# RWKV units of a two-block forward pass: each engine's order laid out over two head pairs, with half-swapped operands

## Chip, cores and metric

One core of one Trainium2 chip. The metric is the device time of one launch in microseconds (us); lower is better. Engines are named as in the profile: PE is TensorE (PEld its weight loads), DVE VectorE, ACT ScalarE, POOL GpSimd, SP SyncE.

## What is computed

The launch runs two transformer-like blocks of two layers each on 512 positions of width 1024, in float32: attention layers first, then a block with an HGRN mixer, an RWKV-7 mixer, a Fourier mixer, a convolution and feed-forward layers. The change touches the RWKV-7 recurrence alone, 8 heads of width 64, run forward and backward in time:

```python
def step(state, inp):
    r_t, w_t, k_t, v_t, a_t, b_t = inp
    sa = jnp.einsum('bhvk,bhk->bhv', state, a_t)
    state = (state * w_t[:, :, None, :] + sa[..., None] * b_t[:, :, None, :]
             + v_t[..., None] * k_t[:, :, None, :])
    return state, jnp.einsum('bhvk,bhk->bhv', state, r_t)
...
for d, (wd, ad, reverse) in enumerate(((wd_f, ad_f, False), (wd_b, ad_b, True))):
    w = -jax.nn.softplus(-(w0[d] + jnp.tanh(wd) @ w2[d])) - 0.5
    decay = jnp.exp(-jnp.exp(heads(w)))
    a = jax.nn.sigmoid(heads(a0[d] + ad @ a2[d]))
    k_d = k_h * (1.0 + (a - 1.0) * k_a_h)
    args = (r_h, decay, k_d, v_h, -kk, kk * a)
    ...
    bonus = bonus + jnp.sum(r_h * k_d * r_k32, axis=-1, keepdims=True) * v_h
```

## The kernel before

The recurrence is cut into chunks of 64 positions. Inside a chunk it becomes a triangular system, which is solved with an inverse that is built by doubling; between chunks it becomes a chain of 8 small state steps. `rwkv_units` does the part inside the chunks, once for each direction d (tiles named ru0 for d = 0, ru1 for d = 1; the profile leaves the numbers out), and `rwkv_states` runs the chain after it. Each call of `rwkv_units` is a stage of its own, with a barrier before and after, and loops over four head pairs (PAIRS = 4). A tile holds one pair: 128 partitions are two halves of 64, and what stands in a half changes with the step: the two heads (index e), or the even and odd chunk of four chunk pairs (index j for the half, t for the chunk pair). Almost every matmul has 64x64 weights, so it uses one quarter of the array: input half times output half. Each float32 matmul leaves two records in the trace.

The steps for one pair, with the function that issues them and its line:

- **turn** (L2555, PE): transposes of the three operands ar, b and kd into banks 0, 1 and 2; **naturals** (L2722, L2726, L2728, ACT) copies them out.
- **scores** (L2568, PE): products of keys and receptances; **masks** (L2785, DVE) multiplies them with the causal masks into `sc`, in two parts k = 0 and k = 1; after part 0 comes the seed of the inverse, a predicated copy (L2792) and a 32x32-block transpose (L2796). `inv` holds the inverse twice: `inv[:, slot, 0]` transposed, `inv[:, slot, 1]` plain.
- **keyed_values** (L2580, PE), copied out by ACT at L2762.
- **level** 1 to 5 (LEVELS = 6): for both heads e, the factors (L2596, PE) are copied out by **taking** (L2717, ACT); the blocks (L2611, PE) multiply that copy with the inverse, in two products k = 0 and k = 1 (level 5 has only one); **adding** (L2805, DVE) puts them into `inv` where the level's mask allows it. The next level's factors need it. This ring PE, ACT, PE, DVE is the heart of a pair.
- **solve** (L2625, PE), copied by **results** (L2733, ACT); **reads** (L2643, PE) with **reading** (L2816, DVE) and **values** (L2737, ACT); **maps** (L2661, PE) with **offsets** (L2744, ACT) and **stepping** (L2822, DVE).
- The class `Decays` prepares the operands of the next pair meanwhile: **lows** (L2348, PE, four records), **tanhs** (L2357, ACT), **sums** (L2384 and the scan L2386, DVE), **difference** (L2393, DVE), **powers** (L2366, L2367, L2371, ACT), **keys** (L2409, L2410, L2412, DVE), **operands** (L2418, L2419, L2421, DVE), and **others** (L2401, L2430 or L2432, L2435, L2436, L2440, L2441, POOL).

Every engine's queue runs in the order in which the block functions write it; a wait holds back all that is behind it. Before the change, PE's order for pair i is turn(i), scores(i), solve(i-1), lows(next), keyed_values(i), level 1, reads(i-1), level 2, maps(i-1), levels 3 to 5. Thus only solve, reads and maps of the pair before stand inside a pair; turn, scores, masks and seed come at its front, with no level in flight. The last pair's solve, reads and maps follow after the loop.

## Time and profile before

| | us |
|---|---|
| median of 3 runs | 2653.24 (2646.54 to 2654.29) |
| profiled execution, its own time | 2654.18 |
| its span | 2652.3 |
| PE busy in the span | 2507.2 (95%) |
| DVE busy | 1564.7 (59%) |
| ACT busy | 958.9 (36%) |
| POOL busy | 326.6 (12%) |

How to read it: the span runs from the first to the last instruction, and the time of the run lies 1.9 us above it. The busy shares are means over all stages of the launch; the RWKV units are two stretches of about 120 us each, from 1356 to 1490 us and from 1503 to 1622 us of the span. A matmul's end in the trace is modelled, so PE's pace is read from the distance between starts.

### The profile page before, as it was taken

How to read it: one execution, taken by the hardware profiler on the slowest of the kernel's cores; microseconds unless marked ns; L12 is line 12 of the kernel's file. 1: busy time of each engine (PE TensorE's matmuls, PEld its weight loads, DVE VectorE, ACT ScalarE, POOL GpSimd, SP SyncE). 2: the span in 40 equal slices, each digit the busy share in tenths (PEclk: the TensorE clock that was granted, in tenths of full speed). 3: DMA queues.
4: the chain of work that ended last, by engine and by line, in shares of the span. 5: the costliest groups of instructions: out<-in, count | busy, mean ns of one | idle time of the engine just before them, and what ended most of it. 6: DMA issues, size and time to landing. Idle time of an engine off the chain costs nothing. (4 is left out here: it accounts for less than half of the span.)

```text
span 2652.3 us, 43599 instructions
## 1 busy us (share of the span) xinstructions
PE 2507.2 (95%) x18620; PEld 1987.2 (75%) x18620; DVE 1564.7 (59%) x2236; ACT 958.9 (36%) x1435; POOL 326.6 (12%) x255
## 2 busy tenths in 40 slices
PE   6999999999999999999889797999999998999998
PEld 5888766678887666788668785788878766788786
DVE  5375378753753787656456565955556696655532
ACT  5223224542232245543444243433322423433321
POOL 1000030030000300300242220300003101100011
PEclk9999999999999999999889998999999998999999
DMA  4333223133332231222100001432334212222231
GB/s 152 96 95 96 97 96 133 56 116 98 100 95 97 96 120 68 102 95 96 62 5 4 3 4 61 179 99 99 118 153 183 64 58 72 88 96 96 84 127 51
DMA packets 56992, 239.38 MB, mean 90 GB/s; under 512 B 6560, under 2 KB 7328, under 8 KB 48224
## 3 DMA queue, kind: packets, MB, share of 16 engines
q1 hardware_dynamic: 56800, 236.61, 25.6%
q8 instruction: 147, 2.41, 0.4%
q14 instruction: 45, 0.37, 0.0%
HBM read 232.39 MB, written 4.19 MB: 89 GB/s over the span
## 5 line engine op out<-in xcount | busy, mean ns | idle before, releaser
L471 PE MATMUL banks<-h,head 128*128 128x512 f32 x1776 | 415.5, 390 | 0.0
L471 PEld LDWEIGHTS banks<-h,head 128*128 128x128 f32 x1776 | 333.1, 188 | 68.8
L471 PE MATMUL banks<-h,pin_pair 128*128 128x512 f32 x1488 | 345.2, 391 | 0.0
L471 PEld LDWEIGHTS banks<-h,pin_pair 128*128 128x128 f32 x1488 | 278.5, 188 | 57.2
L471 PE MATMUL banks<-h,ff_pair 128*128 128x512 f32 x1296 | 298.3, 390 | 0.0
L471 PEld LDWEIGHTS banks<-h,ff_pair 128*128 128x128 f32 x1296 | 243.4, 188 | 50.3
L458 DVE TENSOR_TENSOR head<-first,head 128x1024 fp32r<-128x1024 f32 x74 | 90.5, 1223 | 106.6 <-ACT head L450 106.6
L3163 DVE TENSOR_TENSOR ff<-ff_c,ff 128x512 fp32r<-128x512 f32 x42 | 29.1, 692 | 203.3 <-ACT ff L3151 203.3
L471 PE MATMUL banks<-h,pab_pair 128*128 128x512 f32 x504 | 116.2, 390 | 0.0
L450 ACT ACTIVATE head<-first 128x1024 fp32r<-128x1024 f32 x74 | 78.3, 1058 | 91.9 <-PE banks L471 91.9
L471 PEld LDWEIGHTS banks<-h,pab_pair 128*128 128x128 f32 x504 | 94.6, 188 | 19.6
L458 DVE TENSOR_TENSOR pin_pair<-first,pin_pair 128x1024 fp32r<-128x1024 f32 x34 | 41.7, 1226 | 90.7 <-ACT pin_pair L450 90.7
L1444 DVE SCALAR_TENSOR_TENSOR x<-banks,modf,x 128x512 f32<-128x512 f32 x28 | 21.0, 749 | 114.5 <-PE banks L490 114.5
L458 DVE TENSOR_TENSOR pin_pair<-pin_raw,pin_pair 128x1024 fp32r<-128x1024 f32 x32 | 39.2, 1226 | 79.5 <-ACT pin_pair L450 79.5
L2805 DVE COPY_PREDICATED ru_inv<-b_rp,banks 128x512 f32<-128x512 uint32 (+1 forms) x80 | 53.4, 674 | 51.9 <-PE banks L2611 51.7
L3391 DVE SCALAR_TENSOR_TENSOR cd_acc<-b_hb,params,cd_acc 128x512 f32<-128x512 f32 x108 | 81.2, 752 | 3.6
L990 ACT ACTIVATE dil_pt<-banks 128x1024 f32<-128x1024 f32 x32 | 32.3, 1023 | 140.2 <-PE banks L861 109.4
L490 PE MATMUL banks<-ff,dn_low 128*128 128x512 f32 x352 | 82.4, 389 | 0.0
L207 POOL TENSOR_TENSOR acc<-dn_sq 128x512 f32<-128x512 f32 x2 | 9.3, 4672 | 564.8 <-ACT dn_sq L195 564.8
L490 PEld LDWEIGHTS banks<-ff,dn_low 128*128 128x128 f32 x352 | 66.1, 188 | 13.7
L406 PE MATMUL banks<-h,head 128*128 128x512 f32 x144 | 44.8, 454 | 28.4 <-PEq L70 28.4
L792 POOL MEMSET dil_negmax<- 96x512 bf16 x2 | 1.0, 521 | 569.0 <-POOLq L70 569.0
(590 smaller groups left out, 4910.2 us busy)
## 6 DMA issues: line engine op xcount, KB each, us to landing
first<-in_w_in SPq DMA_DIRECT2D x64, 512.0 KB, 3.5
first<-in_ffn_up SPq DMA_DIRECT2D x56, 512.0 KB, 3.7
dn_raw<-in_ffn_down SPq DMA_DIRECT2D x16, 1408.0 KB, 7.2
dil_ring<-in_ada_w SPq DMA_DIRECT2D x20, 1024.0 KB, 6.9
pin_raw<-in_w_in SPq DMA_DIRECT2D x32, 512.0 KB, 3.5
ff_raw<-in_ffn_up SPq DMA_DIRECT2D x28, 512.0 KB, 3.7
mla_ada_ring<-in_ada_w SPq DMA_DIRECT2D x12, 1024.0 KB, 9.2
first<-in_ab_in SPq DMA_DIRECT2D x22, 512.0 KB, 3.3
```

Source lines behind the costliest of these rows:

```text
L207: self.nc.gpsimd.tensor_tensor(self.m.acc[:, n], self.sq[:, 0, n] if k == 1 else self.m.acc[:, n], self.sq[:, k % 2, n], ALU.add).then_inc ...
L406: mm = nc.tensor.matmul(m.ps[:, 0], pair[0][a][:, k], self.to[:, b, k], start=k == 0 and i == 0, stop=k == KD - 1 and i == 2, skip_group_c ...
L450: nc.scalar.activation(pair[t % slots][0], ring.at(t), ACT.Copy).then_inc(rounded, 1)
L458: nc.vector.tensor_tensor(pair[t % slots][1], ring.at(t), pair[t % slots][0].bitcast(F32), ALU.subtract).then_inc(split, 1)
L471: mm = nc.tensor.matmul(bank, w(a, k), x(b, k), start=k == 0 and i == 0, stop=k == kt - 1 and i == 2)
L490: mm = nc.tensor.matmul(bank, w(1, k), x(0, k), start=False, stop=k == kt - 1)
L792: nc.gpsimd.memset(m.negmax[:], 0.0).then_inc(zeroed, 1)
L990: nc.scalar.activation(pt[:, s:s + 2], m.ps[:, s:s + 2], ACT.Exp, scale=scale)\
L1444: ins = nc.vector.scalar_tensor_tensor(m.x[:, j], m.ps[:, j % 4], gate[:, j:j + 1], m.x[:, j], ALU.mult, ALU.add)
L2805: nc.vector.copy_predicated(inv[:, i % 2, f:2, e], over(m.levels[:, d, l, f:2]), m.ps[:, 4 + e, 2 * f * P:].rearrange("p (k t n) -> p k t ...
L3163: chain.step(nc.vector.tensor_tensor(ff[:, 1, j], cv[:, j % 2], ff[:, 0, j].bitcast(F32), ALU.subtract))
L3391: ins = nc.vector.scalar_tensor_tensor(acc[:, k], hb[:, k, tap:tap + T], w[:, 4 * tap + k:4 * tap + k + 1], acc[:, k], ALU.mult, ALU.add)
```

## The change

It leaves the numbers of instructions of most steps as they are and does five things.

1. It splits `level` into `factors` and `blocks`, `turn` into two calls, and `masks` into its two parts, and writes every engine's order anew. PE's order for pair i is now lows(next), factors 1, solve(i-1), blocks 1, turn of ar and b, factors 2, turn of kd, keyed_values, blocks 2, factors 3, reads(i-1), blocks 3, maps(i-1), factors 4, blocks 4, factors 5, scores(i+1), blocks 5. scores(0) stands ahead of the loop.
2. Factors, keyed_values and solve read one half and write the other (`halves(1 - j)`). Blocks take product 0 from half s to half s and product 1 from half s to the other half r, in turn, where before both went from a half to the same half.
3. For that, ACT copies the seed into the swapped half (`cross`, two instructions of 64 partitions) and `naturals` copies ar in two instructions of 64 partitions instead of one of 128. The seed is made in `m.acc`; POOL's fill is half as large.
4. The banks of PSUM are given out anew: scores in 0 to 3, turn in 0 to 2, reads in 0 and 1, maps in 2 and 3, the levels in 4 to 7.
5. POOL's `others` waits for the tiles' release (turn, reading, diagonal) only behind its first two instructions; scores waits for the first two of POOL's five counts, turn for all five.

The core of the diff:

```diff
             nc.gpsimd.tensor_tensor(self.kds[:, i], self.kds[:, i], self.kd[:], ALU.add).then_inc(self.pooled, 1)
         pool.wait_ge(self.powered, 4 * n + 1)
+        if freed is not None:
+            freed()
...
+                        def freed():
+                            pool.wait_ge(turned, 3 * i + 3)
+                            if i >= 1:
+                                pool.wait_ge(readx, 2 * i - 1)
+                                pool.wait_ge(diag, i)
+
+                        dc.others(pool, i + first, *following(i), (i + 1) % 2, freed)
...
+                def turn(i, some):
                     if i + first:
                         pe.wait_ge(dc.ready, 3 * (i + first))
                         pe.wait_ge(dc.pooled, 5 * (i + first))
-                    if i == 0 and first:
...
                 def scores(i):
+                    if i + first:
+                        pe.wait_ge(dc.ready, 3 * (i + first))
+                    if i + first:
+                        pe.wait_ge(dc.pooled, 5 * (i + first - 1) + 2)
+                    if i == 0 and first:
+                        pe.wait_ge(dc.opened, 2)
                     if i >= 1:
-                        pe.wait_ge(added, 2 * (LEVELS - 1) * i)
+                        pe.wait_ge(natural, 4 * i)
+                        pe.wait_ge(akvx, i)
+                    if i >= 2:
+                        pe.wait_ge(readx, 2 * (i - 1))
+                        pe.wait_ge(qsx, i - 1)
+                        pe.wait_ge(ptx, i - 1)
...
+                def blocks(i, l):
+                    done = 2 * (LEVELS - 1) * i + 2 * (l - 1)
                     if l == 1:
-                        pe.wait_ge(akvx, i + 1)
+                        pe.wait_ge(crossed, 2 * i + 2)
                     for e in range(2):
                         pe.wait_ge(taken, done + e + 1)
-                        for k in range(2 if l < LEVELS - 1 else 1):
-                            for t in range(TT):
+                        for t in range(TT):
+                            at = 2 * P + t * RC
+                            for k in range(2 if l < LEVELS - 1 else 1):
                                 for j in range(2):
-                                    r = halves(j)
-                                    b, back = a1[r, e, t], inv[r, i % 2, 1, e, t]
-                                    lhs, rhs = ((b, back), (back, b))[k]
-                                    at = (1 - k) * 2 * P + t * RC
-                                    mm = nc.tensor.matmul(m.ps[r, 4 + e, at:at + RC], lhs, rhs,
-                                                          start=k == 0 and t == 0, stop=t == TT - 1,
-                                                          skip_group_check=True)
+                                    r, s = halves(j), halves(1 - j)
+                                    b, back = a1[s, e, t], inv[s, i % 2, 1, e, t]
+                                    if k == 0:
+                                        mm = nc.tensor.matmul(m.ps[s, 5 + 2 * e, at:at + RC], b, back, start=False,
+                                                              stop=t == TT - 1, skip_group_check=True)
+                                    else:
+                                        mm = nc.tensor.matmul(m.ps[r, 4 + 2 * e, at:at + RC], back, b, start=t == 0,
+                                                              stop=t == TT - 1, skip_group_check=True)
                         mm.then_inc(paired, 1)
 
                 def solve(i):
                     pe.wait_ge(added, 2 * (LEVELS - 1) * (i + 1))
                     pe.wait_ge(akvx, i + 1)
...
-                                r = halves(j)
-                                mm = nc.tensor.matmul(m.ps[r, 3 - e, t * P:t * P + P], inv[r, i % 2, 1, e, t],
-                                                      x[r, i % 2, e, t], start=t == 0, stop=t == TT - 1,
+                                s = halves(1 - j)
+                                mm = nc.tensor.matmul(m.ps[halves(j), 3 - e, t * P:t * P + P], inv[s, i % 2, 1, e, t],
+                                                      x[s, i % 2, e, t], start=t == 0, stop=t == TT - 1,
                                                       skip_group_check=True)
                         mm.then_inc(solved, 1)
...
                             .then_inc(gated, 1)
+                scores(0)
                 for i in range(PAIRS):
-                    turn(i)
+                    if following(i):
+                        pe.wait_ge(masked, 4 * i + 2)
+                        dc.lows(pe, *following(i), low_banks)
                     if d == 0 and i == 0:
                         pe.wait_ge(placed, PAIRS)
-                    scores(i)
+                    factors(i, 1)
+                    pe.wait_ge(masked, 4 * i + 4)
                     if i >= 1:
                         solve(i - 1)
+                    blocks(i, 1)
                     if following(i):
-                        pe.wait_ge(natural, 3 * i + 2)
-                        dc.lows(pe, *following(i), low_banks)
+                        pe.wait_ge(dc.opened, 2 * (i + first) + 2)
+                    natures = list(enumerate((dc.ar[:, 0], dc.b, dc.kd[:])))
+                    turn(i, natures[:2])
+                    factors(i, 2)
+                    if i >= 1:
+                        pe.wait_ge(wun, 2 * i)
+                    turn(i, natures[2:])
                     keyed_values(i)
-                    level(i, 1)
+                    blocks(i, 2)
+                    factors(i, 3)
                     if i >= 1:
                         reads(i - 1)
-                    level(i, 2)
+                    blocks(i, 3)
                     if i >= 1:
-                        pe.wait_ge(natural, 3 * i + 2)
-                        if following(i):
-                            pe.wait_ge(dc.opened, 2 * (i + first) + 2)
                         maps(i - 1)
-                    for l in range(3, LEVELS):
-                        level(i, l)
+                    for l in range(4, LEVELS):
+                        factors(i, l)
+                        if l == LEVELS - 1 and i < PAIRS - 1:
+                            scores(i + 1)
+                        blocks(i, l)
                 solve(PAIRS - 1)
                 if d == 1:
...
+                def cross(i):
+                    act.wait_ge(seed, i + 1)
+                    if i >= 2:
+                        act.wait_ge(solved, 2 * (i - 1))
+                    for j in range(2):
+                        nc.scalar.activation(inv[halves(1 - j), i % 2, 1], seeds(i)[halves(j)], ACT.Copy)\
+                            .then_inc(crossed, 1)
+
                 def results(i):
...
                         results(i - 1)
                     if following(i):
-                        dc.tanhs(act, i + first, *following(i), low_banks)
-                    act.wait_ge(akved, i + 1)
-                    nc.scalar.activation(x[:, i % 2, :, :, DH:], m.ps[:, 5].rearrange(
-                        "p (e t n) -> p e t n", e=2, t=TT), ACT.Copy).then_inc(akvx, 1)
-                    taking(i, 1)
-                    if following(i):
                         dc.powers(act, i + first, 0)
                     taking(i, 2)
+                    naturals(i)
+                    act.wait_ge(akved, i + 1)
+                    nc.scalar.activation(x[:, i % 2, :, :, DH:], m.ps[:, 3].rearrange(
+                        "p (e t n) -> p e t n", e=2, t=TT), ACT.Copy).then_inc(akvx, 1)
+                    taking(i, 3)
                     if following(i):
                         dc.powers(act, i + first, 1)
                     if i >= 1:
                         values(i - 1)
                         offsets(i - 1)
-                    for l in range(3, LEVELS):
+                    for l in range(4, LEVELS):
                         taking(i, l)
...
 
                 if d == 0:
                     prepare(0, 0, 0, 0)
+                masks(0, 0)
                 for i in range(PAIRS):
                     n, then = i + first, following(i)
-                    masks(i)
+                    masks(i, 1)
                     if then:
                         dc.sums(dve, n, then[0])
                     adding(i, 1)
                     if then:
+                        dc.difference(dve, n)
                         dve.wait_ge(turned, 3 * i + 3)
-                        dc.difference(dve, n)
                         dc.keys(dve, n, then[1])
-                    if i >= 1:
-                        reading(i - 1)
                     adding(i, 2)
                     if then:
                         dc.operands(dve, n, then[1], (i + 1) % 2)
                     adding(i, 3)
                     if i >= 1:
+                        reading(i - 1)
                         stepping(i - 1)
                     for l in range(4, LEVELS):
                         if d == 1 and i == PAIRS - 1:
                             weight(2 * (l - 4))
                             weight(2 * (l - 4) + 1)
+                        if l == LEVELS - 1 and i < PAIRS - 1:
+                            masks(i + 1, 0)
                         adding(i, l)
                 if d == 1:
                     bonus(0)
```

## Rows read from the trace of the kernel before

**Rows 1.** Windows ru0, ru1: length; busy PE, PEld, DVE, ACT, POOL; PEclk, DMA, GB/s.

```profile
1370.40:1490.20 119.80, 106.81 (x3136) 95.11 (x3136) 74.15 (x108) 46.94 (x96) 33.76 (x31) 0.98 0.01 3
...
1502.90:1621.90 119.00, 106.47 (x3140) 93.78 (x3140) 74.51 (x107) 43.06 (x90) 30.77 (x26) 1.00 0.02 4
```

**Rows 2.** Timeline, PE (start, duration): factors 5 of pairs 0 and 3; ru1's first work.

```profile
1394.15 0.33 PE L2596 MATMUL banks<-ru_inv,ru_sc 64*64 64x64 f32 x4
...
1477.84 0.33 PE L2596 MATMUL banks<-ru_inv,ru_sc 64*64 64x64 f32 x4
...
1502.98 0.30 PE L2555 MATMUL banks<-ident,rx_ar 128*128 128x128 f32 x1 [2.73 <-PEq L70]
...
1525.06 0.33 PE L2596 MATMUL banks<-ru_inv,ru_sc 64*64 64x64 f32 x4
...
1608.13 0.28 PE L2596 MATMUL banks<-ru_inv,ru_sc 64*64 64x64 f32 x2 [0.76 <-DVE ru_inv L2805]
```

**Rows 3.** Timeline, three engines: the ring of level 4, pair 0 of ru0.

```profile
1391.00 1.29 PE L2596 MATMUL banks<-ru_inv,ru_sc 64*64 64x64 f32 x32 [0.42 <-DVE ru_inv L2805]
...
1391.73 0.38 ACT L2717 ACTIVATE ru_a<-banks 128x256 f32<-128x256 f32 x1 [2.67 <-PE banks L2596]
...
1392.16 0.68 PE L2611 MATMUL banks<-ru_inv,ru_a 64*64 64x64 f32 x16
...
1392.68 0.63 PE L2611 MATMUL banks<-ru_a,ru_inv 64*64 64x64 f32 x16
...
1393.14 0.63 PE L2611 MATMUL banks<-ru_inv,ru_a 64*64 64x64 f32 x16
1393.36 0.73 DVE L2805 COPY_PREDICATED ru_inv<-b_rp,banks 128x512 f32<-128x512 uint32 x1 [1.80 <-PE banks L2611]
```

**Rows 4.** Timeline, PE: pair 1 of ru1, turn, scores, solve, lows.

```profile
1527.76 0.66 PE L2555 MATMUL banks<-ident,rx_ar 128*128 128x128 f32 x4
...
1529.22 1.10 PE L2568 MATMUL banks<-rx_ar,rx_bb 64*64 64x128 f32 x32
...
1531.02 1.93 PE L2625 MATMUL banks<-ru_x,ru_inv 64*64 64x128 f32 x32
1532.87 1.98 PE L2348 MATMUL banks<-b_rr,b_rp 64*128 64x512 f32 x4
```

**Rows 5.** Timeline, DVE: the same pair, masks, transpose, keys to reading, one of operands.

```profile
1530.39 1.29 DVE L2785 TENSOR_TENSOR ru_sc<-banks,b_rp 128x512 f32<-128x512 f32 x2 [2.07 <-PE banks L2568]
...
1532.48 0.71 DVE L2796 STREAM_TRANSPOSE ru_inv<-ru_inv 128x512 f32<-128x512 f32 x1
...
1540.34 0.68 DVE L2409 SCALAR_TENSOR_TENSOR x<-x,b_rp 128x512 f32<-128x512 f32 x1
...
1542.12 0.68 DVE L2816 TENSOR_TENSOR rx_rp<-banks,rx_ar 128x512 f32<-128x512 f32 x1
...
1545.69 1.75 DVE L2419 SCALAR_TENSOR_TENSOR rx_bb<-x 128x512 f32<-128x512 f32 x1
```

**Rows 6.** Timeline, POOL: beside that one of operands.

```profile
1545.18 1.71 POOL L2435 TENSOR_TENSOR rx_ar<-b_rr,x 128x512 f32<-128x512 f32 x1
```

**Rows 7.** Timeline, ACT: the same pair, offsets and the takings behind it.

```profile
1546.46 0.60 ACT L2744 ACTIVATE rx_qs<-banks 128x512 f32<-128x512 f32 x1 [1.34 <-PE banks L2661]
1546.96 0.81 ACT L2717 ACTIVATE ru_a<-banks 128x256 f32<-128x256 f32 x2
```

**Rows 8.** Timeline, PE: start of the last reads (96 records), start of what follows.

```profile
1614.94 0.46 PE L2643 MATMUL banks<-ru_sc,ru_wu 64*64 64x64 f32 x16
...
1616.50 0.70 PE L2672 MATMUL banks<-rw_kds,b_rp 128*128 128x512 f32 x1
```

**Rows 9.** Timeline: the front of ru0, last operand, scores, first mask.

```profile
1366.09 1.75 DVE L2421 SCALAR_TENSOR_TENSOR rx_ar<-x,b_rp 128x512 f32<-128x512 f32 x1
...
1373.15 1.99 PE L2568 MATMUL banks<-rx_ar,rx_bb 64*64 64x128 f32 x32
...
1375.20 1.29 DVE L2785 TENSOR_TENSOR ru_sc<-banks,b_rp 128x512 f32<-128x512 f32 x2 [7.37 <-PE banks L2568]
```

More of the change, by code:

```diff
@@ L2548, in turn @@
                         pe.wait_ge(dc.pooled, 5 * (i + first))
[L2549 to L2553 removed]
+                    for j, v in some:
                         for t in range(TT):
@@ L2584, in keyed_values, with factors @@
                     mm.then_inc(akved, 1)
-                def level(i, l):
+                def factors(i, l):
                     done = 2 * (LEVELS - 1) * i + 2 * (l - 1)
@@ L2671, in dots @@
                             pe.wait_ge(bonused, i - 1)
-                        nc.tensor.matmul(m.ps[:, 6 + i % 2], m.blocks, dc.kds[:, i], start=True, stop=True)\
+                        nc.tensor.matmul(m.ps[:, 5 + 2 * (i % 2)], m.blocks, dc.kds[:, i], start=True, stop=True)\
                             .then_inc(dotted, 1)
@@ L2755, in _ @@
                 for i in range(PAIRS):
-                    naturals(i)
+                    cross(i)
+                    if following(i):
+                        dc.tanhs(act, i + first, *following(i), low_banks)
+                    taking(i, 1)
                     if i >= 1:
```

95 lines of the change are left out of this document (43 added, 52 removed).

## The prediction, made before the changed kernel ran

> **What bounds the kernel now.** I read the windows by stage first, then the timeline of one level, then that of one pair. In both unit stages PE has work in flight for 107 of 119 us, its granted clock is 0.98 and 1.00 of full speed, and DMA is idle at 3 to 4 GB/s [rows 1]. So no transfer is waited for here, none will be met by work that comes earlier, and what these stages lose the launch loses. PE's share overstates its use: matmuls' ends are modelled, and from one start to the next there are gaps. The distance between factors 5 of pair 0 and of pair 3 is 1477.84 - 1394.15 = 83.7 us in ru0 and 1608.13 - 1525.06 = 83.1 us in ru1 [rows 2], so one pair costs 27.9 or 27.7 us. That period is what the change has to shorten.
>
> One level is a ring [rows 3]: factors start at 1391.00; ACT's taking 0.73 later; blocks 0.43 after that; adding 1.20 after the blocks; the next factors 0.79 after adding (1394.15 [rows 2]). Together 3.15 us. Of the 1.20, 0.93 is the pace of one head's blocks: each run of 16 records takes 0.46 us (1392.68 to 1393.14), there are two, and 0.27 is the hand-over. Five rings are about 16 of the 27.8 us. The rest is the front of a pair, turn at 1527.76 to factors 1, and solve, reads and maps of the pair before. In the front the ring stands still: turn 1.46, scores' first mask 1.17 after its start, then 2.09 to the transpose [rows 4, 5].
>
> **The sum, part by part.**
>
> *Blocks.* Products 0 and 1 of a head now use all four quarters of the array in turn, where both used the same two. The price of four in flight comes from reads: 96 records of the same shape in 1.56 us, 16 ns each, against 29 ns in the blocks [rows 8, 3]. 32 records then take 0.47 instead of 0.93, and adding stands 0.73 after the blocks' start. Level 5 has one product and gains nothing. PE issues 4 levels x 2 heads x 0.46 = 3.7 us less in a pair; on the ring of a level it is 0.46.
>
> *Order, a middle pair laid out by hand.* Zero is factors 5 of the pair before. DVE starts the second head's adding 0.65 after the first, so factors of that head start at 0.65 and scores at 1.1. First mask 1.17 later, 2.3; transpose 2.09 later, 4.4; the two short addings of level 5 behind it, 5.0 and 5.5; masks of part 1, 5.9 and 6.5, and PE sees them 0.7 later, 7.2. Lows (four records, 1.8 us) and factors 1 lie under that from 3.8 to 6.5. Solve 7.2 to 9.1 (1.85 [rows 4]). Blocks 1, 9.1 to 10.0; turn of two operands at 0.49 each to 10.9; factors 2 to 11.9; turn of kd to 12.3; keyed_values, 32 records like factors, to 13.3; blocks 2 at 13.3. DVE may start keys only behind kd's turn, 12.6, and needs 1.78 for them (1540.34 to 1542.12 [rows 5]), so adding 2 stands at 14.4, not 14.0. Factors 3 at 15.2, its second head ends 16.3; reads 1.5 to 17.7; blocks 3; adding 3 at 18.5 and 19.1; reading 19.8; values on ACT 0.8 behind, 20.5; offsets 21.1; taking 21.6 (0.50 apart [rows 7]); blocks 4 at 22.0; adding 22.7; factors 5 at 23.5. Maps (1.5 us from 18.6) end at 20.1 and factors 4 at 21.0, both under the ACT chain. Period **23.5 us**.
>
> Gain: ru0 83.7 - 70.5 = 13.2. ru1 83.1 - 70.5 = 12.6, less 0.7, since its last pair has four bonus products on DVE, two of them (0.6 each, less 0.6 of slack) ahead of adding 4: 11.9.
>
> *Front of ru1.* PE starts at 1502.98 and reaches factors 5 after 22.1 us [rows 2]. New: scores at 0, mask 1.2, transpose 3.3, lows 2.5 to 4.3, factors 1 at 4.3. ACT has two crossings and two tanhs first (0.5 to 0.6 each, from 3.3), so taking 1 is at 5.5, blocks 1 at 5.9, turns to 7.8, factors 2, kd, keyed_values, blocks 2 at 10.1. Keys run 9.5 to 11.2, adding 2 at 11.2, factors 3 at 12.0. Operands are charged 3.0 us, as one of them takes 1.75 beside POOL's 1.71 [rows 5, 6]: 12.5 to 15.5; factors 4 at 16.3, blocks 4 at 17.5, factors 5 at 19.0. Gain 3.1.
>
> *Front of ru0.* Turn waits now until the window's edge, 1370.4 [rows 1], for POOL's fifth count. The new scores need the last operand, which ends at 1366.09 + 1.75 = 1367.8 [rows 9], and go at 1367.9. PE's clock is at half rate there: the first mask stands 2.05 behind scores, not 1.17 [rows 9], and lows lose about as much; I charge 2.0. Factors 5 at 1367.9 + 19.0 + 2.0 = 1388.9 instead of 1394.15: gain 5.2. If the clock stays low for the whole front it is 3; if the shorter gap keeps it high, 7.
>
> *What costs nothing, and under what.* The crossing (two ACT instructions of up to 0.6) ends at about 5.6 and blocks 1 wants it at 9.1; without that cover, in pair 0, it is in the sum above. No row shows an ACT copy of 64 partitions: bounds 0.38, a taking of 256 columns, and 0.60, 512 columns of 128 partitions; I take 0.60, as the columns are 512 [rows 3, 7]. One more instruction in naturals lies between taking 2 and taking 3, where ACT has 3 us free. Adding reads two banks instead of one: price between 0 and 0.1 us; I take 0, 0.73 being one of 512 columns whatever their place. POOL's fill falls from 1024 to 512 columns, off the path. POOL's later instructions wait for reading at 20.5, ar ends near 22.2, and the next scores want it at 24.6: 2.4 us of slack. The tails stay, save 0.2 in ru0.
>
> *Sum.* 13.2 + 11.9 + 3.1 + 5.2 + 0.2 = 33.6 us. Against the profiled execution's 2654.2 that gives 2620.6, said as **2620**; the median shown, 2653.2, lies 1 us under that execution.
>
> *A rule against the change.* Solve has both halves' products in one bank: its 32 records of 128 columns take 1.85 us, 58 ns each, while scores' 64 records of that shape, in four quarters, take 1.80, 28 ns each [rows 4]. So two halves run side by side though they share a bank. The Trainium skill (TensorEngine Tiling (Array Packing), Restrictions and Gotchas) says that row tiles cannot access one PSUM bank at the same time. The trace disagrees for other output partitions. The new blocks keep both halves in one bank for each product; by that rule quarters would not pair and the result would be the first rival's.
>
> **The rivals.**
>
> 1. *Blocks do not speed up*: their pace stays 29 ns, held by the bank that product 0 of both halves shares, while the new order works. For: no row shows three or four quarters with both halves in one bank; reads give each half its own. Against: solve, above. In the layout adding 2 moves 1.0 later (blocks 2 start at 14.2), adding 3 by 1.5, taking 4 by 1.8, factors 5 by 2.3. A period of 25.8: 6 x 2.3 + 2 x 1.5 = 17 us less gain, **2637**.
> 2. *POOL gets in DVE's way elsewhere.* Operands are free of POOL now, but its late instructions (ar, decay, b and kd, some 5 us) stand beside the seed and transpose of the next pair. A shared stretch costs up to 1.1 us [rows 5, 6]; 8 pairs, **2629**.
> 3. *Crossed matmuls do not overlap*: from half 0 to half 1 and back they run one at a time. Place: factors (160 records a pair), keyed_values (32), product 1 of blocks (128) at +24 ns each, and solve (32) at +50 ns: 9.3 us a pair, 74 us, **2694**: slower. Against: scores' 28 ns and reads' 16 ns need all four quarters at once. It decides from 4.2 us a pair, the gain: if crossed records cost 13 ns more.
> 4. *The new order does not take hold*: scores of the next pair stand behind a late producer, so blocks 5 wait and the ring stands still as before. ar would have to be 4.2 + 2.4 = 6.6 us late; then **2653**, no change.
> 5. *Better than laid out*: operands of pair 0 without POOL, a clock that stays high in ru0's front, offsets off the ring: 1.2 + 2 + 0.8 x 6, **2612**.
>
> **How the numbers follow.** A measurement of this kernel can tell about 0.3%, 8 us, from no change. Chances: the forecast 0.66, rival 1 0.11, rival 2 0.12, rival 5 0.05, together faster 0.94; rival 4 0.02 for the same; rival 3 0.04 for slower. The forecast's own range is 2613 to 2628, some 1 us a pair either way. The whole reaches from rival 5 to rival 1: 2608 to 2638, which leaves out rivals 3 and 4 and some of the tails.
>
> **What would show it.** Factors 5 to factors 5, pairs 0 to 3: 70 us in each stage, 77 by rival 1. Blocks of one head: 32 records in 0.47 us, adding 0.73 behind their start. Masks ahead of addings of level 5 on DVE, scores at 1.1 after factors 5. Solve about 7 us after factors 5; if it stands at 9, masks of part 1 are dearer than laid out. DVE ahead of adding 2 should wait for nothing, ahead of taking 4 ACT should come from offsets. Prediction wrong if factors take over 1.1 us for 32 records, or if the stages outside shift by other than what the two stages give.

## The result, and the profile after it

The changed kernel takes 2633.86 us (median of 6 runs, 2628.59 to 2638.19) against 2650.70 us (6 runs, 2646.54 to 2654.29) of the kernel before on the same chip: a ratio of 0.9937, 95% interval 0.9918 to 0.9955. That is **16.8 us faster**. The forecast was 2620 us, a gain of 33.6; its range, 2608 to 2638, holds the result. The sign was right, and half of the gain was missing. The result lies outside the forecast's own range, 2613 to 2628; only the upper end that was set for rival 1 reaches it, and rival 1's mechanism did not come. That the whole range holds the result is luck.

The profiled execution took 2630.05 us (span 2628.1). The windows of the two stages, ru0 from its opening barrier on and ru1 as in [rows 1], with the columns of [rows 1]:

```profile
1357.10:1478.00 120.90, 100.37 (x3148) 82.17 (x3148) 77.88 (x117) 60.30 (x119) 36.95 (x38) 0.96 0.02 6
1490.20:1603.30 113.10, 94.40 (x3140) 81.65 (x3140) 69.89 (x107) 50.14 (x102) 26.53 (x26) 0.97 0.02 4
```

From the end of one barrier to the end of the next, ru0 went from 134.1 us (1356.0 to 1490.1) to 120.8 (1357.2 to 1478.0), and ru1 from 119.3 (1502.6 to 1621.9) to 113.1: 13.3 and 6.2 us. PE does the same matmuls, and its busy time is 12 us smaller in ru1 than in [rows 1], because more of them overlap; but the stage became only 6 us shorter. So PE waits more than before (in ru1 18.7 us against 12.5), and the question is for what.

Factors 5 of pairs 0 to 3 (before: [rows 2]) now start at 1388.61, 1413.74, 1440.15, 1466.23 in ru0 and at 1510.25, 1535.49, 1559.96, 1588.64 in ru1. From pair 0 to pair 3 that is 77.6 us instead of 83.7, and 78.4 instead of 83.1. The layout said 70.5 (71.2 in ru1, with its 0.7 us for the bonus products).

**One pair, step by step.** The second pair of ru1 is the layout's middle pair; zero is 1510.25. PE, then DVE, then ACT (start, duration, instruction, count, and in brackets the idle time ahead with what ended it):

```profile
1510.25 1.11 PE L2608 MATMUL banks<-ru_inv,ru_sc 64*64 64x64 f32 x26 [0.25 <-DVE ru_inv L2844]
1511.15 0.32 PE L2580 MATMUL banks<-rx_ar,rx_bb 64*64 64x128 f32 x1
...
1516.00 1.15 PE L2608 MATMUL banks<-ru_inv,ru_sc 64*64 64x64 f32 x32
1517.17 1.64 PE L2641 MATMUL banks<-ru_x,ru_inv 64*64 64x128 f32 x26
```

```profile
1512.48 1.29 DVE L2825 TENSOR_TENSOR ru_sc<-banks,b_rp 128x512 f32<-128x512 f32 x2 [1.68 <-PE banks L2580]
...
1514.58 0.71 DVE L2836 STREAM_TRANSPOSE ru_inv<-acc 128x512 f32<-128x512 f32 x1
1515.21 0.73 DVE L2844 COPY_PREDICATED ru_inv<-b_rp,banks 128x256 f32<-128x256 uint32 x2
1515.85 1.27 DVE L2825 TENSOR_TENSOR ru_sc<-banks,b_rp 128x512 f32<-128x512 f32 x2
...
1524.59 1.33 DVE L2844 COPY_PREDICATED ru_inv<-b_rp,banks 128x512 f32<-128x512 uint32 x2
1525.82 0.76 DVE L2418 TENSOR_TENSOR rx_kb<-rx_kd,x 128x512 f32<-128x512 f32 x1
...
1529.45 1.35 DVE L2844 COPY_PREDICATED ru_inv<-b_rp,banks 128x512 f32<-128x512 uint32 x2 [1.11 <-PE banks L2629]
1530.70 0.66 DVE L2855 TENSOR_TENSOR rx_rp<-banks,rx_ar 128x512 f32<-128x512 f32 x1
...
1534.71 1.34 DVE L2844 COPY_PREDICATED ru_inv<-b_rp,banks 128x512 f32<-128x512 uint32 x2 [0.29 <-PE banks L2629]
```

```profile
1531.40 0.60 ACT L2776 ACTIVATE rx_y<-banks 128x512 f32<-128x512 f32 x1 [3.27 <-DVE rx_rp L2855]
1533.02 0.60 ACT L2783 ACTIVATE rx_qs<-banks 128x512 f32<-128x512 f32 x1 [1.02 <-PE banks L2680]
```

| step | laid out | measured |
|---|---|---|
| scores, first mask, transpose | 1.1, 2.3, 4.4 | 0.9, 2.2, 4.3 |
| masks of part 1, solve | 5.9, 7.2 | 5.6, 6.9 |
| adding 2 | 14.4 | 14.3 |
| adding 3 | 18.5 | 19.2 |
| reading | 19.8 | 20.5 |
| offsets | 21.1 | 22.8 |
| adding 4 | 22.7 | 24.5 |
| factors 5 | 23.5 | 25.2 |

Up to adding 2 the pair runs as laid out, to 0.3 us. All that is missing is lost behind it, and offsets wait for PE's maps (L2680), not for DVE as the layout had it.

**What PE waits for.** The waits of PE (engine, tile, line, releaser: sum in us, times, longest) from factors 5 of pair 0 to those of pair 3 in ru0. First the kernel before, then the changed one:

```profile
PE banks L2596 <- issue: 1.8, 2, 1.2
PE banks L2596 <- DVE ru_inv L2805: 1.6, 6, 0.4
PE banks L2661 <- issue: 1.6, 2, 0.9
PE banks L2611 <- issue: 0.5, 2, 0.3
```

```profile
PE banks L2608 <- issue: 2.6, 2, 1.3
PE banks L2629 <- issue: 2.5, 2, 1.5
PE banks L2608 <- DVE ru_inv L2844: 2.4, 5, 0.6
PE banks L2680 <- issue: 1.8, 1, 1.8
PE banks L2626 <- issue: 1.0, 1, 1.0
```

"Issue" is time in which PE waits for nothing that the profile shows: 7.9 us in six waits, 2.6 us a pair (6.6 us in ru1, also in six). 77.6 less 7.9 is 69.7, the layout's 70.5 to 0.8 us. The kernel before had 3.9 us of it in its three periods. These waits stand in the middle of steps that wait for no semaphore, as here within the blocks of level 3:

```profile
1432.30 0.22 PE L2629 MATMUL banks<-ru_a,ru_inv 64*64 64x64 f32 x1
...
1434.06 0.27 PE L2629 MATMUL banks<-ru_a,ru_inv 64*64 64x64 f32 x1 [1.54 <-issue]
...
1437.62 0.27 PE L2608 MATMUL banks<-ru_inv,ru_sc 64*64 64x64 f32 x3 [1.32 <-issue]
```

**Where they stand.** The profile's third part has the queues:

```profile
q8 instruction: 147, 2.41, 0.4%
```

147 packets with 2.41 MB are 16 KB each. PE has 37,836 instructions in the trace (weight loads, matmuls, semaphore events and drains, with 24 matmuls whose records are missing), and that is 147.8 times 256: so q8 is PE's queue, with 256 instructions of 64 bytes in a packet. Counted through the trace, PE's records come to a multiple of 256 between unexplained gaps. This list is worked out from the trace: start of each packet of q8, and each gap between two starts on PE of more than 1.1 us, with the index of the record ahead of it modulo 256.

```
packet 1402.06   packet 1405.89   gap 1407.09 to 1408.26, mod 168
packet 1409.50                    gap 1410.60 to 1412.10, mod 168
packet 1431.71                    gap 1432.30 to 1434.06, mod 168
packet 1435.29                    gap 1436.09 to 1437.62, mod 168
packet 1457.08                    gap 1458.13 to 1459.34, mod 168
packet 1460.53                    gap 1461.26 to 1463.24, mod 168
```

Six gaps in different steps, all at the same remainder. It is not only these: between factors 5 of pairs 0 and 3, in both stages, the traces of all fourteen runs of this case (the kernel before among them) hold 118 waits of PE on "issue", and every one stands at remainder 168 where 24 matmul records are missing (18,596 of 18,620 in the trace after) and at 192 where none is. The 24 are the difference. A gap ends 2.3 to 2.7 us after the start of a packet (2.2 to 3.0 over the 118), and in no place of this launch does a packet follow the one before in less than 3.37 us (in the list, 3.45; over all traces, 3.2). The reading: PE executes instructions that arrive in blocks of 256, and from factors 3 to blocks 4 it asks for them faster than they come.

One pair has about 1,568 PE instructions (factors 5 x 64, blocks 4 x 128 + 64, scores 128, solve 64, reads 192, maps 192, and some 100 others); reads, blocks 3, maps, factors 4 and blocks 4 are 704 of them (a float32 matmul is four: two weight loads, two matmuls), which the layout puts between 16.2 and 23.0, in 7 us. At 256 in 3.5 us they need 9.6. The whole pair would need only 21.4 us at that rate, less than the layout's 23.5, so the shortage is local. Nothing is stored up for the dense stretch: counted the same way, a packet of the changed kernel starts when PE has at most 300 instructions left before the block that it carries, 260 in the median, which is about one block.

This is told in the Trainium skill (Runtime: NRT & Kernel Launch, Instruction fetch mechanics) as blocks of 16 KiB with 256 instructions, whose crossing is "mostly hidden". This trace agrees on the blocks. On the hiding it agrees in part: of the 18 crossings in the 77.6 us of ru0, twelve show no wait, and six cost 7.9 us together.

### The profile page after: what moved, and what is told of

It reads as the page before. It is cut to its first block and busy times, and to the rows that moved or that the text cites. A ratio compares the mean times of both kernels' runs of the same rounds, so it can differ in the third digit from the quotient of the medians.

```text
span 2628.1 us, 43653 instructions
## 1 busy us (share of the span) xinstructions
PE 2468.0 (94%) x18596; PEld 1951.8 (74%) x18620; DVE 1555.2 (59%) x2236; ACT 972.8 (37%) x1459; POOL 320.3 (12%) x255
## 3 DMA queue, kind: packets, MB, share of 16 engines
q1 hardware_dynamic: 56800, 236.61, 26.1%
q8 instruction: 147, 2.41, 0.4%
## 5 line engine op out<-in xcount | busy, mean ns | idle before, releaser
L450 ACT ACTIVATE head<-first 128x1024 fp32r<-128x1024 f32 x74 | 78.3, 1058 | 91.6 <-PE banks L471 91.6
L471 PEld LDWEIGHTS banks<-h,pab_pair 128*128 128x128 f32 x504 | 94.5, 188 | 19.6
L450 ACT ACTIVATE ff_pair<-first 128x1024 fp32r<-128x1024 f32 x30 | 32.0, 1065 | 100.3 <-PE banks L471 89.7
```

The source lines that it names most:

```text
L450: nc.scalar.activation(pair[t % slots][0], ring.at(t), ACT.Copy).then_inc(rounded, 1)
L471: mm = nc.tensor.matmul(bank, w(a, k), x(b, k), start=k == 0 and i == 0, stop=k == kt - 1 and i == 2)
```

## The experiments

The theories, as they stood ahead of the runs. **A**: PE's supply of instructions sets the pace between factors 3 and blocks 4. **B**: the matmuls of the blocks get in each other's way in the banks, so the gaps belong to those matmuls. **C**: a hand-over between engines was misjudged; for e11 and e12 this is told as a wait that belongs to the maps or to the reads. **D** (for e6): interleaving the products of the blocks is worth nothing in any case. **E** (for e7): the half-rate clock in ru1's last pair comes from PE's idle wait at its front. All distances are from factors 5 of pair 0 to those of pair 3, ru0 / ru1; the changed kernel has 77.6 / 78.4, and in two repeats 75.9 / 78.3 and 75.7 / 77.9. So a distance in ru0 is known to 2 us. The "issue" waits of those three executions are 7.9, 6.3 and 5.8 us in ru0, and what is left of the distance without them is 69.7, 69.6 and 69.9: the scatter in ru0 is the supply's. The rest of e2, which computes the same, is 68.8, so the rest is known to about 1 us. The table gives both for every run; its last two columns are the sum of PE's "issue" waits in the stretch and the distance without them.

| ru0, pair 0 to 3 | distance | issue | rest |
|---|---|---|---|
| changed kernel, e5, e10 | 77.6, 75.9, 75.7 | 7.9, 6.3, 5.8 | 69.7, 69.6, 69.9 |
| e7, filler (ru1 only) | 77.0 | 7.3 | 69.7 |
| e2, padding | 74.5 | 5.7 | 68.8 |
| e1, long reads and maps | 71.2 | 0 | 71.2 |
| e11, long reads | 72.9 | 2.3 | 70.6 |
| e12, long maps | 70.9 | 1.0 | 69.9 |
| e3, product order | 77.2 | 5.6 | 71.6 |
| e6, long, product order | 73.1 | 0 | 73.1 |
| e4, maps late | 75.4 | 2.9 | 72.5 |
| e9, maps late | 75.7 | 3.8 | 71.9 |
| e8, split lows | 83.8 | 6.2 | 77.6 |

The subtraction is an account, not an experiment: a wait taken away may let another show, as in e1, where the rest is 71.2 with no wait on "issue" left.

A run's total says less: from factors 5 of ru1's last pair to the end, code that no experiment touches, single executions took 1039.1 to 1045.4 us. For experiments with a single execution the distances are read, not the totals.

### e1: reads and maps as four long matmuls

```diff
 def reads(i):
-    for t in range(TT): ... 48 matmuls of 64x64
+    for j in range(2):
+        mm = nc.tensor.matmul(m.ps[:, j, 0:448], m.ident[:], wu[:, j]...[:, 0:448], start=True, stop=True)
 def maps(i):
-    for t in range(TT): ... 48 matmuls of 64x64
+    for j in range(2): (the same, from ben and ken into banks 2 and 3)
```

This leaves out what reads and maps compute; they take about their time (1.77 us for the reads, where the short ones take 1.57) and keep their places, waits and signals.

> Reads and maps (192 PE instructions each) are replaced by two 448-column matmuls each (8 instructions, about the same PE time); their results are left out. Theory A (PE runs out of instructions: they come in blocks of 256, one per 3.5 us at best, and a level-3 stretch uses 640 in 8.5 us): the unexplained PE gaps inside blocks and maps vanish, factors 5 of pair 0 to pair 3 in ru0 falls from 77.6 to 70.5 to 71.5 us, the layout's value. Theory B (quarter-array matmuls collide in PSUM banks, the gap is an execution stall of blocks): gaps inside blocks 3 stay, the distance falls by the gaps in maps only, to about 74 us. Theory C (a hand-over was misjudged): 77 us, no change.

2627.31 us. Distances **71.2 / 73.6**; the periods in ru0 are 23.72, 23.73 and 23.73 us, the layout's 23.5 to 0.2. PE's waits in the same stretch of ru0:

```profile
PE banks L2608 <- DVE ru_inv L2822: 2.8, 6, 0.6
PE banks L2626 <- ACT ru_a L2725: 0.5, 3, 0.2
```

No wait on "issue" is left, and the ring's own waits are nearly as they were (2.8 us for DVE, where it was 2.4 to 2.8 in the changed kernel). That is what A said; B had 74 us and C 77.

### e11, e12: only the reads, only the maps

> Only the reads are replaced by two 448-column matmuls (their results are left out of what is computed), the maps are as in the changed kernel: a pair issues 188 instructions fewer than the changed kernel's 1568, half of what e1 saved. Theory A (PE's supply of instructions, 256 per 3.5 us at best, runs short only between factors 3 and blocks 4): that stretch then needs some 450 instructions, 6.2 us of supply against 8 us of work, so periods of 23.7 to 24.3 us in ru0, distance 71 to 73 us, and the gaps at one place of the instruction stream go or shrink under 0.5 us each. Rival (the ring is held by the maps' wait for ACT and DVE, not by supply): periods stay at 25 to 26 us, distance 75 to 77.

> Only the maps are replaced by two 448-column matmuls (their results are left out), the reads are as in the changed kernel: again 188 instructions fewer in a pair. Theory A: the same as with the reads replaced, 71 to 73 us in ru0. Rival (the reads and what waits for them set the pace): 75 to 77 us, while replacing the reads alone would give 71.

Distances 72.9 / 73.3 with the reads replaced and **70.9 / 73.6** with the maps replaced. In ru0 the maps alone give all of e1's gain and the reads alone about two thirds (2.8 to 4.7 us of 4.5 to 6.4), as a supply that runs short only locally would; a wait that belongs to maps alone would have stayed with long reads, and one that belongs to reads with long maps. Waits of PE in ru0, e11 and then e12:

```profile
PE banks L2608 <- DVE ru_inv L2833: 3.2, 7, 0.6
PE banks L2669 <- issue: 1.4, 1, 1.4
PE banks L2608 <- issue: 0.9, 1, 0.9
PE banks L2626 <- ACT ru_a L2736: 0.6, 1, 0.6
```

```profile
PE banks L2608 <- DVE ru_inv L2833: 2.8, 6, 0.6
PE banks L2629 <- issue: 1.0, 1, 1.0
PE banks L2626 <- ACT ru_a L2736: 0.3, 2, 0.2
```

The 5.8 to 7.9 us of "issue" became 2.3 and 1.0. "Under 0.5 us each" was too much to expect: one or two gaps stay.

### e2: 128 waits ahead of the first scores

```diff
     pe.wait_ge(g2_in, 16)
+    for _ in range(128):
+        pe.wait_ge(g2_in, 16)
```

The waits are fulfilled already. In the trace they stand as 64 records with two waits each, so they move all that follows by 64 instructions, a quarter of a block, and not by the 128 of the expectation.

> 128 extra waits that are already satisfied, on PE, once, ahead of the first scores of ru0. Nothing else moves. Theory A: the gaps without a releaser stand every 256 instructions of PE, so all of them from there on move by 128 instructions in the program and keep their count modulo 256 (168 in the trace of the changed kernel); they hit other steps, the sum over a pair stays within 1 us. Theories B and C: the gaps stay at the same matmuls of the program. The extra waits cost 3 to 8 us once, at the front of ru0.

2631.53 us; distances 74.5 / 76.7. All eleven waits on "issue" in the two stages are again at one remainder (192, with no record missing, the padding counted). So each gap now stands 64 instructions earlier in the program. The four over 1.1 us in ru0's pairs are at 1409.35 (1.54), 1412.80 (1.80), 1437.04 (1.41) and 1460.85 (1.20): in the first period they stand 18.0 and 21.5 us behind factors 5, where they were 18.5 and 22.0. Three of the waits are now within maps (L2680), where there was one, and none is left in factors (L2608), where there were two. The gaps go with the count and not with a matmul, as A said and against B and C.

The padding itself takes PE's queue 6.8 us, 106 ns for each record (1359.02 to 1365.79), and holds the next matmuls back:

```profile
1365.90 5.46 PE L2700 MATMUL banks<-b_rr,rx_y 128*128 128x512 f32 x6 [5.66 <-issue]
```

The front of ru0 grew by 4.1 us (from the barrier to factors 5 35.4 instead of 31.3), since part of the 6.8 lies where PE waited for its operands anyway.

### e3, e6: the products one after the other

```diff
-    for t in range(TT):
-        for k in range(2 if l < LEVELS - 1 else 1):
+    for k in range(2 if l < LEVELS - 1 else 1):
+        for t in range(TT):
```

e3 undoes the order of the loops alone; the swapped halves stay. e6 does it together with e1's edit (and leaves out the same).

> Blocks' loops put back with product outside and chunk pair inside, so that two of the four quarters work at a time; all else as in the changed kernel. All theories: one head's blocks take 0.93 instead of 0.5 us and adding stands 1.20 instead of 0.75 behind their start. Theory A: PE uses instructions more slowly, so part of the 1.7 us of gaps in a pair is given back: factors 5, pair 0 to 3 of ru0, rises from 77.6 by 3 x 0.5 to 3 x 1.2, to 79 to 81 us; the kernel 4 to 9 us slower than the changed one. Theories B and C: by 3 x 2.3, to 84 to 85 us, 17 us slower than the changed kernel, about level with the kernel before.

> Reads and maps as in e1 (two long matmuls each, results left out) and blocks' product order as in e3. Under the instruction limit the order of the products was worth nothing (77.6 and 77.2 us). Theory A: without the limit it is worth what the layout says, 2 to 2.3 us a pair: distance in ru0 77 to 78 us against 71.2 in e1. Theory D (the order of products is worth nothing in any case, since DVE sets the pace): 71 to 72 us.

e3: 2633.04 us, ratio to before 0.9932 (0.9913 to 0.9951), distances 77.2 / 77.3. Level with the changed kernel, where A had 79 to 81 us in ru0 and the other theories 84 to 85: **under the limit the interleaved products are worth nothing that shows**. The table has the reason: the rest grows by 1.8 us, 0.6 a pair, but a slower ring asks for fewer instructions at a time, and the waits on "issue" are 5.6 us instead of 5.8 to 7.9.

e6: 2622.34 us; 73.1 / 74.5, with periods of 24.37, 24.37 and 24.38 us, against 23.73 in e1. Without the limit they are worth 0.65 us a pair. The two differences agree. A, by the layout, had 2 to 2.3; D had nothing; both missed. Part of A's miss is that the edit does not bring the old pace back: the 64 records of blocks 4 take 1.35 us in e6, 21 ns each, against 1.82 us (29 ns) in the kernel before and 0.94 us (15 ns) in e1. With the swapped halves the second product starts among the records of the first (L2629 from 1434.47, L2626 from 1434.18). So the two runs price the order of the loops, not the whole step from two quarters to four.

### e4: maps behind blocks 4

```diff
     blocks(i, 3)
-    if i >= 1:
-        maps(i - 1)
     for l in range(4, LEVELS):
...
         blocks(i, l)
+        if l == 4 and i >= 1:
+            maps(i - 1)
```

ACT's values and offsets go behind taking 4, DVE's stepping behind adding 4.

> Maps of the pair before behind blocks 4 instead of behind blocks 3, values and offsets on ACT behind taking 4, stepping on DVE behind adding 4. Theory A: the stretch from factors 3 to blocks 4 now uses 448 instructions in some 6.5 us, so its gaps shrink; by the layout a pair is 23.7 us; I expect 24.0 to 24.8 instead of 25.9 in ru0 (distance 72 to 75) and the kernel 6 to 12 us faster than the changed one. Theories B and C: gaps stay with the steps that have them, and a pair gets 0.2 longer by the layout: distance 78, the kernel level with the changed one.

2632.54 us, ratio 0.9932 (0.9917 to 0.9948); 75.4 / 77.7. Against the repeats of the changed kernel, 75.7 and 75.9, nothing is gained, where 6 to 12 us were expected. The table splits it: in ru0 the waits on "issue" did fall, to 2.9 us, and the rest rose by 2.7, to 72.5 (one stretch of 3.4 us at half rate, at 1408.1, is in it; e9, with the same order and none in ru0's pairs, has 71.9). 1.4 us of that is a new wait, of the next pair's scores for DVE's late stepping:

```profile
PE banks L2580 <- DVE rx_pt L2861: 1.4, 2, 0.7
```

That the other half is maps in the way of the ring of levels 4 and 5 is not shown. In ru1 the waits on "issue" fell only to 5.6 us, from 6.3 to 7.0 in the changed kernel. So the supply was relieved mainly in ru0, and the order spent what it gave.

### e8: lows as sixteen short matmuls

```diff
-    dc.lows(pe, *following(i), low_banks)
+    for j, v in enumerate((dc.w2, dc.a2)):
+        for n in range(8): (the same product, 64 columns at a time)
```

> Lows as sixteen 64-column matmuls instead of two of 512 columns: 64 PE instructions instead of 8 in a pair, at about the same PE time, in a stretch (scores to solve) that uses only some 50 instructions per us. Theory A, with instructions fetched ahead only for a block or two: 0 to 0.8 us a pair, distance in ru0 77.6 to 80, and the gaps again at one remainder modulo 256, shifted from pair to pair otherwise. Theory B: no change, 77.6, gaps at the same matmuls as in the changed kernel.

2654.15 us; 83.8 / 88.8. The distance does not tell the theories apart, since the step itself grew. It was four records in 1.98 us, and in e8's timeline of PE it is:

```profile
1394.02 3.98 PE L2707 MATMUL banks<-b_rr,b_rp 64*128 64x64 f32 x32
```

Its 32 records start 112 ns apart, and the clock fell more often: three stretches at half rate within the pairs of ru0 and three within those of ru1, where the changed kernel has none and one. The places of the gaps do tell something: with 56 instructions more in each pair, all eleven waits on "issue" of the two stages are again at one remainder (168), and in ru0 they fall in maps (L2680, two), factors (L2608, one) and blocks (L2626, two), not at the matmuls of the changed kernel as B had it.

### e7, e9: filler work in the last pair of ru1; e5, e10: the changed kernel again

```diff
     if following(i):
         ... lows
+    else:
+        pe.wait_ge(masked, 4 * i + 2)
+        for j, v in enumerate((dc.w2, dc.a2)):
+            nc.tensor.matmul(low_banks[j], v[halves(d), 0:P], rr[halves(d), 12 + j], start=True, stop=True)
```

The period that ends ru1's pairs is longer than the others. Windows of the three periods of the changed kernel, columns as in [rows 1]:

```profile
1510.25:1535.49 25.24, 22.10 (x784) 19.41 (x784) 17.05 (x28) 13.27 (x27) 6.78 (x8) 1.00 0.02 4
1535.49:1559.96 24.47, 21.89 (x783) 19.29 (x784) 17.00 (x27) 13.27 (x27) 7.76 (x9) 1.00 0.02 4
1559.96:1588.64 28.68, 22.27 (x781) 20.52 (x780) 13.38 (x21) 10.12 (x21) 2.38 (x2) 0.93 0.02 4
```

The granted clock is 0.93 in the third: one stretch of 3.4 us from 1567.8 is at the lower level, 1.2 GHz, behind a time in which PE, with no lows to do, waited 1.6 us for DVE:

```profile
1565.90 1.15 PE L2608 MATMUL banks<-ru_inv,ru_sc 64*64 64x64 f32 x32 [1.59 <-DVE ru_inv L2844]
1567.31 2.00 PE L2641 MATMUL banks<-ru_x,ru_inv 64*64 64x128 f32 x20 [0.27 <-DVE ru_sc L2825]
```

Solve behind it has 20 records in 2.00 us, against 26 in 1.64 in the pair above. PE's waits over all three periods show the supply as well:

```profile
PE banks L2680 <- issue: 4.5, 3, 1.8
PE banks L2608 <- DVE ru_inv L2844: 4.1, 7, 1.6
PE banks L2629 <- issue: 2.1, 3, 0.8
PE banks L2641 <- DVE ru_sc L2825: 0.3, 1, 0.3
```

> In the last pair of ru1, which has no lows, two 512-column matmuls of the same shape are put in lows' place, into banks that nobody reads; all else as in the changed kernel. Theory E (the half clock in ru1's fourth pair comes from PE's idle stretch at its front): no half-clock stretch between pair 2 and 3, fourth pair 25.5 to 26.5 us instead of 28.7, the kernel 2 to 3 us faster than the changed one. Against it: the stretch comes and goes between executions, then level with it.

> Both earlier edits together: the maps go behind the fourth blocks (which shortened factors 5 of pair 0 to pair 3 in e4 from 75.9 to 75.3 us in ru0 and from 78.3 to 77.6 in ru1), and two 512-column matmuls take the place of the level matmuls in the last pair of ru1 (e7: 76.9 in ru1, with no half-clock stretch between its pairs 2 and 3). Theory A (PE's instruction supply sets the pace, the clock adds to it in ru1): the two add up to 2 to 5 us under the changed kernel in the same call, some 2623 to 2626, distances of about 75 and 76 us. Rival (both were scatter of single executions): level with the changed kernel within 1.5 us.

> The changed kernel once more, as the partner of the three others on one chip. Theory A: the gaps without a releaser stand again every 256 PE instructions; distance of factors 5, pair 0 to 3, 76 to 79 us in ru0. In ru1 the fourth pair is 28.7 us in the first trace, with two stretches of 3.4 us at half clock; if these depend on where the clock's windows fall, this trace may show none, and the fourth pair is then about 26.

> The changed kernel itself, as the yardstick of this call: 2628 to 2634 us, distances of 75.5 to 78.4 us, the gaps of PE again at one and the same place of its instruction stream (index modulo 256).

| | us (runs) | ratio to before | ru0 / ru1 |
|---|---|---|---|
| e5, changed kernel | 2627.93 (2627.47 to 2640.94) | 0.9922 (0.9894 to 0.9951) | 75.9 / 78.3 |
| e7, filler | 2627.56 (2624.68 to 2630.68) | 0.9908 (0.9885 to 0.9930) | 77.0 / 76.9 |
| e9, filler and maps late | 2630.73 (2629.86 to 2635.63) | 0.9925 (0.9912 to 0.9938) | 75.7 / 76.5 |
| e10, changed kernel | 2630.94 (2627.45 to 2635.11) | 0.9925 (0.9912 to 0.9938) | 75.7 / 77.9 |

With filler the last period of ru1 is 25.98 us in e7 and 25.78 in e9, and no half-rate stretch lies between its pairs 2 and 3; in the three executions of the changed kernel it is 28.68, 27.84 and 27.86, and one does. That is what E said, but other runs take its cause away. e3 has no filler and the same idle wait for DVE ahead of the same factors, and its clock stays at the upper level:

```profile
1570.38 1.15 PE L2608 MATMUL banks<-ru_inv,ru_sc 64*64 64x64 f32 x32 [1.59 <-DVE ru_inv L2844]
```

```profile
1564.45:1590.75 26.30, 21.61 (x781) 20.00 (x780) 13.39 (x21) 10.11 (x21) 1.42 (x2) 1.00 0.02 4
```

So do e1, e6, e11 and e12 (idle waits of 1.5 to 1.6 us), and in e2, with 1.15 us, the period is 25.97 without filler; e4 and e8 have the stretch. So a half-rate stretch costs this period about 2 us when it comes, and the idle wait alone does not bring it; that the filler keeps it away is not shown. In the total nothing shows: e9 is level with e10, where A had it 2 to 5 us lower. No version tried, of those that compute the whole, is measurably faster than the changed kernel.

## Why the prediction was right, and where it failed

**Middle pair, 23.5 us: the step that failed.** It measured 25.9 in ru0 (77.6 / 3) and 26.1 in ru1. The layout let PE issue reads, blocks 3, maps and factors 4 back to back, since every operand was there, and charged nothing for the instructions themselves; they stall 7.9 us in the three periods of ru0. Take them away (e1) and the period is 23.73, the layout's to 0.2. The missing term is the supply: PE gets 256 instructions in about 3.5 us, with about one block in store. The hint was in the trace of before: 3.9 us of "issue" in the same stretch, of which the prediction says nothing, because the ring of level 4 in [rows 3] has none. The terms 13.2 and 11.9 us became 6.1 and 4.7.

**Blocks, four quarters at once: right in pace, probably over-priced in worth.** Adding stands 0.76 us behind the blocks' start (laid out 0.73; in the last level-4 ring of pair 0 in ru0 blocks start at 1387.06, adding at 1387.82), and the ring of a level is 2.72 us (factors 4 at 1385.89, factors 5 at 1388.61) instead of 3.15:

```profile
1385.89 1.29 PE L2608 MATMUL banks<-ru_inv,ru_sc 64*64 64x64 f32 x32 [1.19 <-DVE ru_inv L2844]
1387.06 0.27 PE L2626 MATMUL banks<-ru_inv,ru_a 64*64 64x64 f32 x2
...
1387.82 1.35 DVE L2844 COPY_PREDICATED ru_inv<-b_rp,banks 128x512 f32<-128x512 uint32 x2 [1.38 <-PE banks L2629]
...
1388.61 1.12 PE L2608 MATMUL banks<-ru_inv,ru_sc 64*64 64x64 f32 x26 [0.25 <-DVE ru_inv L2844]
```

Rival 1 is refuted. Its price, 2.3 us a pair, was laid out for 29 ns a record, which no run with the new order has. What the runs price is 21 ns (e6) against 15 (e1): adding 1 stands at 9.4 us in both, adding 2, behind keys, at 14.5 and 14.4, adding 3 at 19.2 and 18.8, adding 4 at 23.6 and 22.9, the pair 0.65 longer. The layout moved adding 2, ahead of which DVE does keys, by 1.0; it moves by 0.1. Rows with the two halves in one bank run at 17 ns a record, so in this trace two halves with other output partitions do run side by side in one bank, as the prediction had taken from solve.

**Last pair of ru1**: charged 0.7 us for the bonus products; its period is 3.4 us longer than the longer of the other two. The clock was taken as full there, as in [rows 1] (1.00), and in this execution it was 0.93; in runs whose clock stayed full the period is 25.8 to 26.3 us (e2, e3, e7, e9), so about 2 to 3 us are the clock's. What brings the lower level there stays open. The 0.7 itself is 0.6 by the terms that the prediction gives.

**Fronts.** ru1: 19.6 us from PE's first work (1490.63) to factors 5, 19.0 laid out, gain 2.5 for 3.1. ru0: gain 6.7 for 5.2. The 2.0 us charged for a half-rate clock were not needed; the first mask stands 1.17 us behind scores, not 2.05 as in [rows 9]:

```profile
1369.14 1.10 PE L2580 MATMUL banks<-rx_ar,rx_bb 64*64 64x128 f32 x32 [1.53 <-DVE rx_ar L2421]
...
1370.31 1.29 DVE L2825 TENSOR_TENSOR ru_sc<-banks,b_rp 128x512 f32<-128x512 f32 x2 [1.23 <-PE banks L2580]
```

**Small terms.** Copies of 64 partitions take 0.59 to 0.63 us on ACT, near the upper bound that was taken (0.60). Adding from two banks takes 0.71 to 0.75 us for 512 columns, nothing more. The two short addings of level 5 stand at 5.0 and 5.3 us of the pair, laid out 5.0 and 5.5. The tail gave 0.5 us back in ru0 and cost 0.9 in ru1, where the half-rate clock from 1588.3 lies.

**Other rivals.** 2, POOL in DVE's way: operands of the middle pair take 0.68 to 0.76 us each, the seed takes 0.73 to 0.74 us in seven of the eight pairs (1.11 in the first) and the transpose 0.71 in all, and the pair stands as laid out up to adding 2; refuted. 3, crossed matmuls one at a time: factors take 1.1 us for 32 records as before; refuted. 4: scores stand at 0.9, so the order took hold. 5 did not come; its offsets did not come off the ring: they wait for PE's maps.

**The sum.** Expected 13.2 + 11.9 + 3.1 + 5.2 + 0.2 = 33.6. Measured in the profiled execution 6.1 + 4.7 + 2.5 + 6.7 + 0.5 - 0.9 = 19.6, which is the two stages' 13.3 + 6.2 to 0.1. The medians differ by 16.8; the two profiled executions differ by 24.1, the other 4.6 us in stages that are the same in both. The prediction names such a shift as a sign against it; since the medians differ by less than the two stages give, it is read as scatter between single executions and not as a gain of the change.

## What to carry to other kernels

Short matmuls are bound by instructions as well as by waits: count the PE instructions between two points of a layout (four for each float32 matmul) and hold them against the 256 in 3.5 us measured here before trusting a stretch in which all operands are ready. "Issue" waits in the middle of a step, at a constant remainder of the instruction count, are the sign; fewer and longer matmuls there took them away, and moving the same ones did not pay. A few added instructions ahead of the stretch (64 in e2) test it without changing the work: such gaps move with the count. An order that packs waits of other engines under PE's work brings its gain only until that supply is spent, and a ring that gets shorter by itself gains only where nothing else holds its next step.

## What was not expected of the hardware

- Instruction packets of 16 KB for PE came at best 3.4 to 3.6 us apart in the changed kernel (never under 3.2 in any trace), though each took only 0.9 to 1.5 us itself and DMA was idle (4 to 6 GB/s). They start about one block ahead of need (260 instructions in the median, 300 at most). Why not earlier stays open: no run here changes it.
- An instruction with two waits that are fulfilled already costs PE's queue 106 ns (e2, 64 of them).
- 64x128 weights with 64 columns take 112 ns a record on one half of the rows (e8); 512 columns take 0.43 us, and 0.54 for the first record (lows of the changed kernel).
- In the changed kernel a stretch at half rate follows an idle wait of 1.6 us within a pair that is otherwise dense, in all three executions; in e1, e3, e6, e11 and e12 a wait as long stands at the same place and no such stretch follows. So the wait is not enough to tell it.
